# Attention heads on one Trainium2 core: lower weights in half units, probability copies ahead of the exponentials

## The chip, the cores and the metric

The kernel runs on one core of one Trainium2 chip. The metric is the device time of one execution in microseconds (us), and lower is better. TensorE (PE) multiplies, VectorE (DVE), ScalarE (ACT) and GpSimd (POOL) work on elements, SyncE (SP) issues most of the DMA transfers. Each engine takes its own instructions in program order and waits at semaphores for the others.

## The reference, cut to what matters

Two blocks of a network run over 256 tokens of 1024 channels in float32. The first block has a layer with two attentions of 16 heads each, both over the same normalised input. The first adds a forgetting bias to the scores, the second is a mixture of three dilated windows, which the kernel folds into one bias table. Its core is

```python
s = jnp.einsum('bqhd,bkhd->bhqk', q[:, q0:e], k[:, :e]).astype(f32) * scale
s = s + c[:, :, q0:e, None] - c[:, :, None, :e]
p = jax.nn.softmax(jnp.where(causal, s, NEG), axis=-1)
outs.append(jnp.einsum('bhqk,bkhd->bqhd', p.astype(v.dtype), v[:, :e]))
```

for the first one. All other layers (retention, a state space layer, a third attention of 8 heads, a feed-forward layer) are untouched by the change.

## The kernel before, in words

**Weights in two parts.** Float32 weights are multiplied as an upper and a lower part, each of which TensorE can take at full rate. The weights arrive in 232 units of 128x1024 elements (512 KB) in a ring of four buffers, `stage`. ACT copies a unit to `w_hi` with rounding (`split_hi`, line 607) and signals `hi_ready`. DVE subtracts that from the unit to make `w_lo` (`split_lo`, line 892) and signals `lo_ready`. SP loads unit u into a buffer when unit u - 4 has signalled `lo_ready`. TensorE takes three passes over each unit (lines 1507, 1511 and 1515 where the channels come out on the partitions, 1488, 1492 and 1496 where the tokens do), then signals `unit_used`.

**The two attention halves.** `for half in range(2)` runs the first attention and then the second, each with heads 0 to 15 of its own. The order is written out by hand on each engine.
- TensorE (`attend`): at an even head i it makes the scores of heads i + 2 and i + 3 (`scores_of_pair`, lines 1595 and 1596, a wait for `scored` of head i + 1 ahead of it). Then for each head i it turns the probabilities of head i by three transposes (line 1614; it waits for the exponentials of head i and for the copy of head i - 2), and then multiplies the values with the turned probabilities of head i - 1 (lines 1625 to 1627; it waits for the copy of head i - 1).
- DVE: for head i `score_max` adds the bias, writes `prob` and takes the row maximum (lines 1078 and 1079). It copies the turned probabilities of head i - 2 from PSUM into `prob_t` (`copy_prob`, line 1085) unless ACT does that head. At i = 9 and 17 it inverts the denominators, and at i = 11 and 19 it multiplies eight heads with the gate (line 1096), once POOL has scaled that gate (line 468). At i = 4, 8 and 12 it makes one lower unit each.
- ACT: for head n it takes the exponentials in two instructions (lines 708 and 709), and then copies the turned probabilities of head n - 2 if that is one of heads 0, 2, 6 and 10 (`copy_prob_act`, line 717). After head 2 it makes one more upper unit.

The values of the unit ahead of an attention are finished before its first turn. `prob` has three buffers, `prob_t` has two, and `copy_prob_act(n)` also waits until the values of head n - 2 are multiplied.

After an attention half TensorE goes straight on: after the first with the chunks `("qb", c)`, four units each, after the second with the turns of `turn_wide` (line 1444) and the output projection.

Of the kernel before, what the change touches and what calls it, by code (L numbers as in the profile page):

```python
# [20 lines left out]
F32 = mybir.dt.float32  # L21
# [3 lines left out]
ALU = mybir.AluOpType  # L25
# [21 lines left out]
RING = 4  # L47
UNIT = 1024
# [1 line left out]
NC = S // STEP  # L50
AHEAD = 3
DOWN_LAST = 3
SPLIT_HEADS = (4, 8, 12)
COPIED_BY_ACT = (0, 2, 6, 10)
MASKS_AT, TABLES_AT = 20, 42
FORGET_AT, PARAMS_AT = 5, 12
# [77 lines left out]
def build(nc, t):  # L134
    chunks, n_units = weight_chunks()
    number = {name: c[3] for name, c in chunks.items()}
    last_unit = {name: c[0] + c[1] - 1 for name, c in chunks.items()}

    with ExitStack() as ctx:
# [4 lines left out]
        stage = sb("stage", [P, RING, UNIT])  # L144
        w_hi = sb("w_hi", [P, RING, UNIT], F32R)
        w_lo = sb("w_lo", [P, RING, UNIT], F32R)
# [101 lines left out]
        def bank(b, width=BANK, at=0):  # L248
            return ps[:, b * BANK + at:b * BANK + at + width]
# [3 lines left out]
        hi_ready, lo_ready, unit_used = sem("hi_ready"), sem("lo_ready"), sem("unit_used")  # L253
# [38 lines left out]
        def result(name, width=BANK):  # L292
            if name[0] == "down":
                at = (4 + 2 * name[1]) * BANK
                return ps[:, at:at + 2 * BANK].rearrange("p (b n) -> p b n", b=2)
            n = number[name]
            return ps[:, (n % 2) * 2 * BANK:(n % 2) * 2 * BANK + 2 * BANK].rearrange("p (b n) -> p b n", b=2)[:, :, 0:width]

        def chunk_done(eng, name):

            eng.wait_ge(unit_used, last_unit[name] + 1)
# [296 lines left out]
        def _(act):  # L598
            next_unit = [0]
# [10 lines left out]
            def ahead(name):  # L610
                split_hi(last_unit[name] + 1 + AHEAD)
# [74 lines left out]
            for half, kind in enumerate(("ga", "gb")):  # L686
                for c in range(2):
# [3 lines left out]
                    for b in range(NB):  # L691
                        ins = nc.scalar.activation(gate0[half][:, b, c * 512:(c + 1) * 512], result((kind, c))[:, b, :], ACT.Silu, scale=rstd[:, b:b + 1])
# [11 lines left out]
            def exponentials(n):  # L704

                act.wait_ge(scored, n + 1)
                e = prob[:, n % 3, :]
                nc.scalar.activation(e[:, 0:256], e[:, 0:256], ACT.Exp, bias=neg_max[:, 1, n:n + 1], scale=-1.0, accum_out=den[:, 1, n:n + 1])  # L708
                nc.scalar.activation(e[:, 256:384], e[:, 256:384], ACT.Exp, bias=neg_max[:, 0, n:n + 1], scale=-1.0,
                                     accum_out=den[:, 0, n:n + 1]).then_inc(exped, 1)  # L710

            def copy_prob_act(n):

                act.wait_ge(prob_turned, n + 1)
                if n >= 2:
                    act.wait_ge(pv_done, n - 1)
                nc.scalar.activation(prob_t[:, n % 2, :], bank(2 + n % 2, 384), ACT.Copy).then_inc(prob_copied_act, 1)

            for half in range(2):
                v = "va" if half == 0 else "vb"  # L720
                if half == 1:
                    for part in range(2):
                        ahead((("qb", "kb")[part], 1))
                        act.wait_ge(b_turned, part + 1)
                        if part:
                            act.wait_ge(c_pow_ready, 1)
                        for i in range(4):
                            nc.scalar.activation(b_turn[:, 2 * part + i // 2, i % 2], bank(4 + i).rearrange("p (t n) -> p t n", t=CT), ACT.Copy).then_inc(b_ready, 1)
                for c in range(2):
                    if c == 0:  # L730
                        ahead((v, 0))
                    else:
                        split_hi(last_unit[(v, 1)] + AHEAD)
                        exponentials(16 * half)
                        exponentials(16 * half + 1)
                    chunk_done(act, (v, c))
                    for b in range(NB - c):
                        ins = nc.scalar.activation(v0[:, b, c * 512:(c + 1) * 512], result((v, c))[:, b, :], ACT.Copy, scale=rstd[:, b:b + 1])
                    ins.then_inc(drain_sem((v, c)), 1)
                for n in range(16 * half + 2, 16 * half + 16):  # L740
                    exponentials(n)
                    if copied_by_act(n - 2):
                        copy_prob_act(n - 2)
                    if n == 16 * half + 2:
                        ahead((v, 1))
            hi_of_wide(range(4))
# [11 lines left out]
            for c in range(4):  # L758
                ahead(("rv", c))
                chunk_done(act, ("rv", c))  # L760
                for b in range(NB):
                    ins = nc.scalar.activation(v1[:, b, c * 512:(c + 1) * 512], result(("rv", c))[:, b, :], ACT.Copy, scale=rstd[:, 2 + b:3 + b])
                ins.then_inc(drain_sem(("rv", c)), 1)
            for c in range(4):
                ahead(("rg", c))
                chunk_done(act, ("rg", c))
                for b in range(NB):
                    ins = nc.scalar.activation(gate1[:, b, c * 512:(c + 1) * 512], result(("rg", c))[:, b, :], ACT.Silu, scale=rstd[:, 2 + b:3 + b])
# [20 lines left out]
            for b in range(NB):  # L789
                ins = nc.scalar.activation(qkv[:, b, 0:SINK_H, :], result(("sq", 0))[:, b, :].rearrange("p (h d) -> p h d", d=HD), ACT.Copy,  # L790
                                           scale=rstd_in_q[:, b:b + 1])
            ins.then_inc(drain_sem(("sq", 0)), 1)
            chunk_done(act, ("skv", 0))
            for b in range(NB):
# [3 lines left out]
                ins = nc.scalar.activation(qkv[:, b, V_AT:V_AT + KV_H, :], heads[:, KV_H:2 * KV_H, :], ACT.Copy, scale=rstd_in[:, b:b + 1])  # L798
# [45 lines left out]
            for c in range(2):  # L844
                for b in range(NB):
                    act.wait_ge(mixed_ready, 2 * c + b + 1)
                    half = slice(c * 512, (c + 1) * 512)
# [22 lines left out]
            for b in range(NB):  # L870
                ins = nc.scalar.activation(down_out[:, b, 0:512], result(("down", 0))[:, b, :], ACT.Copy, scale=rstd[:, 14 + b:15 + b])
# [13 lines left out]
        def _(dve):  # L885
            next_unit = [0]

            def split_lo(until):

                for u in range(next_unit[0], min(until, n_units)):  # L890
                    dve.wait_ge(hi_ready, u + 1)
                    nc.vector.tensor_tensor(w_lo[:, u % RING, :], stage[:, u % RING, :], w_hi[:, u % RING, :].bitcast(F32), ALU.subtract).then_inc(lo_ready, 1)  # L892
                next_unit[0] = max(next_unit[0], min(until, n_units))

            def ahead(name):
                split_lo(last_unit[name] + 1 + AHEAD)
# [68 lines left out]
            for a in range(2):  # L965
                r = slice(a * SSM_N, (a + 1) * SSM_N)
                ins = nc.vector.tensor_copy(sp["ldt"][r, :], log_dt[r, :].rearrange("p (t a) -> p t a", a=2)[:, :, a])
# [57 lines left out]
            for i, (f0, f1, op) in enumerate(((fr_b, fi_b, ALU.subtract), (fi_b, fr_b, ALU.add))):  # L1025
                TT(b_tmp[0][:], b_in[0][:], f0, ALU.mult)
                then(TT(b_tmp[1][:], b_in[1][:], f1, ALU.mult))
                for a in range(2):
                    r = slice(a * SSM_N, (a + 1) * SSM_N)
                    ins = TT(b_wide[i][r, :, a, :], b_tmp[0][r], b_tmp[1][r], op)  # L1030
# [67 lines left out]
            for half in range(2):  # L1098
                if half == 1:
                    for c in range(2):  # L1100
                        take_heads("qb", q0, c)
                for c in range(2):
                    take_heads(("ka", "kb")[half], k0, c)
                v = (("va", "vb")[half], 1)
                split_lo(last_unit[v] + 1)
                for i in range(16 + 4):
                    n = 16 * half + i
                    if i < 16:
                        score_max(n, half)
                    if i == 1:  # L1110
                        chunk_done(dve, v)
                        TS(v0[:, 1, 512:1024], result(v)[:, 1, :], rstd[:, 1:2], None, ALU.mult).then_inc(v_block_ready, 1)
                    if 2 <= i < 18 and not copied_by_act(n - 2):
                        copy_prob(n - 2)
                    if i % 8 == 1 and i >= 9:
                        invert((n - 9) // 8)
                    if i % 8 == 3 and i >= 11:
                        if n == 35:
                            lo_of_wide(range(1))
                        gate_heads((n - 11) // 8)  # L1120
                    if i in SPLIT_HEADS:
                        split_lo(last_unit[v] + 2 + SPLIT_HEADS.index(i))

            def out_and_turn(kind, n_hi, gain):

# [25 lines left out]
            for kind, dst in (("rq", q1), ("rk", k1)):  # L1151
                for c in range(2):
# [3 lines left out]
                    for hh in range(2):  # L1156
# [5 lines left out]
                        ins = TT(by_sin, src, rot[:, 1, :].unsqueeze(1).to_broadcast([P, 2, S]), ALU.mult)  # L1162
                        then(ins)
                        TT(dst[:, h, 0, :], by_cos[:, 0, :], by_sin[:, 1, :], ALU.subtract)
                        ins = TT(dst[:, h, 1, :], by_sin[:, 0, :], by_cos[:, 1, :], ALU.add)
# [56 lines left out]
            for b in range(NB):  # L1222
                ins = STT(x[:, b, :], x[:, b, :], rstd[:, 4 + b:5 + b], row_a[:], ALU.mult, ALU.mult)
# [42 lines left out]
            for pair in range(2):  # L1266
                chunked = lambda v, m: v.rearrange("p (m n j) -> p m n j", m=m, j=STEP)
                ins = TT(u_p[:, 2 * pair:2 * pair + 2].rearrange("p m j n -> p m n j"), chunked(result(("u", 0))[:, pair, :], 2),
                         chunked(rstd_row[:], 1).to_broadcast([P, 2, NC, STEP]), ALU.mult)
# [32 lines left out]
            for b in range(NB):  # L1302
                ins = TT(y_attn[:, b, :].rearrange("p (h d) -> p h d", d=HD), bank(4 + b).rearrange("p (h d) -> p h d", d=HD),
                         inv_den[:, b, 32:40].unsqueeze(2).to_broadcast([P, SINK_H, HD]), ALU.mult)
# [8 lines left out]
            for c, dst in ((1, gate_z), (0, ssm_out)):  # L1313
                ahead(("glu", c))
                chunk_done(dve, ("glu", c))
                for b in range(NB):
                    ins = TT(dst[:, b, :], result(("glu", c))[:, b, :], row_b[:, c * 512:(c + 1) * 512], ALU.add)
# [83 lines left out]
            for b in range(NB):  # L1401
# [4 lines left out]
                for c in range(2):  # L1406
                    half = slice(c * 512, (c + 1) * 512)
# [539 lines left out]
```

## Time and profile before

| | |
|---|---|
| time, median of 3 runs | 804.79 us |
| lowest and highest | 803.68 and 807.3 us |
| the profiled execution | 803.58 us |
| its span | 801.8 us |
| TensorE busy | 776.6 us (97%) |
| VectorE busy | 519.9 us (65%) |
| ScalarE busy | 406.1 us (51%) |
| GpSimd busy | 218.0 us (27%) |
| granted TensorE clock, mean | 0.996 |

The span is the time from the first to the last instruction that the profiler saw, and the execution's own time has 1.8 us more around it. Busy shares are averages over stages that differ, so what matters for a change is which engine is waited for inside the stage that it touches.

### The profile page before, as it was taken

How to read it: one execution, taken by the hardware profiler on the slowest of the kernel's cores; microseconds unless marked ns; L12 is line 12 of the kernel's file. 1: busy time of each engine (PE TensorE's matmuls, PEld its weight loads, DVE VectorE, ACT ScalarE, POOL GpSimd, SP SyncE). 2: the span in 40 equal slices, each digit the busy share in tenths (PEclk: the TensorE clock that was granted, in tenths of full speed). 3: DMA queues.
4: the chain of work that ended last, by engine and by line, in shares of the span. 5: the costliest groups of instructions: out<-in, count | busy, mean ns of one | idle time of the engine just before them, and what ended most of it. 6: DMA issues, size and time to landing. Idle time of an engine off the chain costs nothing.

```text
span 801.8 us, 12695 instructions
## 1 busy us (share of the span) xinstructions
PE 776.6 (97%) x5133; PEld 678.5 (85%) x5133; DVE 519.9 (65%) x759; ACT 406.1 (51%) x649; POOL 218.0 (27%) x180
## 2 busy tenths in 40 slices
PE   7999999999989999999999999998999999999996
PEld 6879987899878889997777888987887888888885
DVE  4755864775547656875556975686678767677453
ACT  5653436534456445343435454726766655556441
POOL 3031893290531000018007930125102110111010
PEclk9999999999999999999999999999999999999999
DMA  8996993567721463656455466440263666665651
GB/s 217 214 256 205 217 206 106 124 160 180 157 79 58 147 194 109 227 165 184 127 159 160 150 205 197 137 150 7 83 233 122 196 208 189 186 184 179 213 180 53
DMA packets 77821, 130.72 MB, mean 163 GB/s; under 512 B 4414, under 2 KB 28210, under 8 KB 77634
## 3 DMA queue, kind: packets, MB, share of 16 engines
q1 hardware_dynamic: 76418, 125.00, 54.2%
q0 software_dynamic: 1200, 4.83, 2.1%
q8 instruction: 41, 0.67, 0.3%
q14 instruction: 18, 0.15, 0.1%
q10 hardware_dynamic: 144, 0.07, 0.0%
HBM read 128.82 MB, written 1.06 MB: 162 GB/s over the span
## 4 chain that ended last, share of the span: by engine, by line
PE 87%; DVE 4%; ACT 4%; DMA 3%; issue 1%; SPq 0%; POOL 0%; DVEq 0%; POOLq 0%; ACTq 0%
PE ps L1488 13%; PE ps L1492 13%; PE ps L1496 13%; PE ps L1528 10%; PE ps L1507 6%; PE ps L1511 6%; PE ps L1515 6%; PE ps L1532 5%; DMA stage<-in_even_w_in 3%; PE ps L1595 2%; PE ps L1614 1%; DVE w_lo L892 1%; ACT w_hi L607 1%; PE ps L1625 1%; PE ps L1905 1%
## 5 line engine op out<-in xcount | busy, mean ns | idle before, releaser
L892 DVE TENSOR_TENSOR w_lo<-stage,w_hi 128x1024 fp32r<-128x1024 f32 x232 | 303.7, 1327 | 166.3 <-ACT w_hi L607 165.8
L607 ACT ACTIVATE w_hi<-stage 128x1024 fp32r<-128x1024 f32 x232 | 242.6, 1061 | 238.1 <-PE ps L1496 112.3
L1488 PE MATMUL ps<-w_hi,act_t 128*128 128x512 f32 (+1 forms) x376 | 103.3, 398 | 3.3 <-issue 2.8
L1496 PE MATMUL ps<-w_lo,act_t 128*128 128x512 f32 (+1 forms) x376 | 98.6, 385 | 0.0
L1528 PE MATMUL ps<-act_t,w_hi 128*128 128x512 f32 x352 | 88.3, 393 | 0.7 <-DVE act_t L929 0.7
L1488 PEld LDWEIGHTS ps<-w_hi,act_t 128*128 128x128 f32 x376 | 68.6, 190 | 18.7 <-issue 5.8
L1492 PE MATMUL ps<-w_hi,act_t 128*128 128x512 f32 (+1 forms) x312 | 82.2, 387 | 0.0
L1496 PEld LDWEIGHTS ps<-w_lo,act_t 128*128 128x128 f32 x376 | 69.7, 188 | 14.3
L1528 PEld LDWEIGHTS ps<-act_t,w_hi 128*128 128x128 f32 x352 | 63.3, 189 | 12.2 <-issue 0.9
L1492 PEld LDWEIGHTS ps<-w_hi,act_t 128*128 128x128 f32 x312 | 58.2, 190 | 12.1
L1507 PE MATMUL ps<-act_t,w_hi 128*128 128x256 f32 x416 | 58.8, 284 | 0.0
L1511 PE MATMUL ps<-act_t,w_hi 128*128 128x256 f32 x416 | 58.4, 283 | 0.0
L1515 PE MATMUL ps<-act_t,w_lo 128*128 128x256 f32 x416 | 58.4, 283 | 0.0
L1507 PEld LDWEIGHTS ps<-act_t,w_hi 128*128 128x128 f32 x416 | 53.8, 193 | 0.2
L1515 PEld LDWEIGHTS ps<-act_t,w_lo 128*128 128x128 f32 x416 | 53.7, 193 | 0.0
L1511 PEld LDWEIGHTS ps<-act_t,w_hi 128*128 128x128 f32 x416 | 53.7, 193 | 0.0
L1532 PEld LDWEIGHTS ps<-act_t,w_lo 128*128 128x128 f32 x352 | 48.0, 190 | 3.5
L1532 PE MATMUL ps<-act_t,w_lo 128*128 128x256 f32 x352 | 49.1, 282 | 0.0
L584 POOL TENSOR_TENSOR big<-big 128x512 f32<-128x512 f32 x11 | 14.3, 1299 | 105.5 <-ACT big L864 105.5
L1492 PE MATMUL ps<-w_hi,y_lo 128*128 128x512 f32 x128 | 34.2, 389 | 0.0
L708 ACT ACTIVATE prob<-prob,neg_max 128x256 f32<-128x256 f32 x40 | 20.2, 506 | 22.5 <-DVE neg_max L1079 22.3
L1492 PEld LDWEIGHTS ps<-w_hi,y_lo 128*128 128x128 f32 x128 | 24.0, 188 | 5.0
(363 smaller groups left out, 1159.6 us busy)
## 6 DMA issues: line engine op xcount, KB each, us to landing
stage<-in_even_w_in SPq DMA_DIRECT2D x64, 512.0 KB, 5.5
stage<-in_odd_w_in SPq DMA_DIRECT2D x48, 512.0 KB, 4.3
stage<-in_w_gate_up SPq DMA_DIRECT2D x44, 512.0 KB, 4.7
stage<-in_w_down SPq DMA_DIRECT2D x22, 512.0 KB, 4.0
stage<-in_even_w_out SPq DMA_DIRECT2D x16, 512.0 KB, 4.3
stage<-in_odd_w_out SPq DMA_DIRECT2D x16, 512.0 KB, 4.6
stage<-in_w_in SPq DMA_DIRECT2D x10, 512.0 KB, 4.5
stage<-in_w_out SPq DMA_DIRECT2D x8, 512.0 KB, 4.7
```

Of the source, the lines that this page charges most:

```text
L607: nc.scalar.activation(w_hi[:, u % RING, :], stage[:, u % RING, :], ACT.Copy).then_inc(hi_ready, 1)
L708: nc.scalar.activation(e[:, 0:256], e[:, 0:256], ACT.Exp, bias=neg_max[:, 1, n:n + 1], scale=-1.0, accum_out=den[:, 1, n:n + 1])
L892: nc.vector.tensor_tensor(w_lo[:, u % RING, :], stage[:, u % RING, :], w_hi[:, u % RING, :].bitcast(F32), ALU.subtract).then_inc(lo_ready, 1)
L1488: mm(out[:, b, :], a_hi(k)[:, tok[b]], hi[:, i, :], start=(k == 0), stop=False)
L1492: mm(out[:, b, :], a_lo(k)[:, tok[b]], hi[:, i, :], start=False, stop=False)
L1496: ins = mm(out[:, b, :], a_hi(k)[:, tok[b]], lo[:, i, :], start=False, stop=(k == k_tiles - 1))
L1507: mm(out[m], columns(hi[:, i, :], m), act_t[:, k, :], start=(k == 0 and m % 2 == 0), stop=False, skip_group_check=True)
L1511: mm(out[m], columns(hi[:, i, :], m), act_t[:, KD + k, :], start=False, stop=False, skip_group_check=True)
L1515: ins = mm(out[m], columns(lo[:, i, :], m), act_t[:, k, :], start=False, stop=(k == k_tiles - 1), skip_group_check=True)
L1528: mm(out[m], hi[:, i, w[m]], both[:, :, k, :], start=(k == 0), stop=(k == KD - 1), skip_group_check=True)
L1532: ins = mm(out[m][:, 0, :], lo[:, i, w[m]], act_t[:, k, :], start=False, stop=(k == KD - 1), skip_group_check=True)
L1595: even = mm(bank(0, width, at), qs[0][:, tok], ks[0][:, 0:width], start=True, stop=True)
```

## The change

The three whole lower units of each attention half become six half units. Each is 512 of the 1024 columns. They stand at the ends of heads 4, 5, 7, 9, 12 and 13 in place of 4, 8 and 12, and only the second half of a unit signals `lo_ready`. On ACT the copy of head n - 2 moves ahead of the exponentials of head n.

```diff
-SPLIT_HEADS = (4, 8, 12)
+SPLIT_HEADS = (4, 5, 7, 9, 12, 13)
...
                 for n in range(16 * half + 2, 16 * half + 16):
-                    exponentials(n)
                     if copied_by_act(n - 2):
                         copy_prob_act(n - 2)
+                    exponentials(n)
                     if n == 16 * half + 2:
                         ahead((v, 1))
...
+            def split_lo_half(u, part):
+
+                half = slice(part * UNIT // 2, (part + 1) * UNIT // 2)
+                dve.wait_ge(hi_ready, u + 1)
+                ins = nc.vector.tensor_tensor(w_lo[:, u % RING, half], stage[:, u % RING, half], w_hi[:, u % RING, half].bitcast(F32), ALU.subtract)
+                if part == 1:
+                    ins.then_inc(lo_ready, 1)
+                    next_unit[0] = u + 1
...
                     if i in SPLIT_HEADS:
-                        split_lo(last_unit[v] + 2 + SPLIT_HEADS.index(i))
+                        at = SPLIT_HEADS.index(i)
+                        split_lo_half(last_unit[v] + 1 + at // 2, at % 2)
```

## Rows read from the trace of the kernel before

**Rows 1.** The page: its head, and section 4, the chain that ended last.
```profile
span 801.8 us, 12695 instructions
...
PE 87%; DVE 4%; ACT 4%; DMA 3%; issue 1%; SPq 0%; POOL 0%; DVEq 0%; POOLq 0%; ACTq 0%
```

**Rows 2.** Windows: the first attention and what follows; columns PE, PEld, DVE, ACT, POOL.
```profile
131.30:158.70 27.40, 23.77 (x203) 21.01 (x203) 19.80 (x75) 17.77 (x63) 3.69 (x4) 1.00 0.44 97
158.70:231.20 72.50, 72.50 (x522) 67.97 (x522) 39.96 (x38) 30.08 (x40) 38.56 (x25) 1.00 0.65 153
```

**Rows 3.** Waits, 131 to 159 us: total us, times, longest.
```profile
PE ps L1625 <- ACT prob_t L717: 3.6, 4, 1.2
```

**Rows 4.** The chain, 126 to 160 us, first attention: start us, us, what.
```profile
131.31 0.41 PE ps L1595
...
132.20 0.43 PE ps L1614 x3
...
135.17 0.41 PE ps L1595
...
139.02 0.41 PE ps L1595
...
139.88 0.48 PE ps L1614 x3
...
140.97 0.34 PE ps L1614 x3
...
141.96 0.41 PE ps L1595
...
148.75 0.41 PE ps L1595
...
152.84 0.41 PE ps L1595
...
158.67 1.01 PE ps L1507 x8
```

**Rows 5.** Timeline of ACT, 126 to 145 us: start us, us, instruction, idle before.
```profile
132.87 0.51 ACT L708 ACTIVATE prob<-prob,neg_max 128x256 f32<-128x256 f32 x1 [0.84 <-DVE neg_max L1079]
...
134.13 1.04 ACT L607 ACTIVATE w_hi<-stage 128x1024 fp32r<-128x1024 f32 x1
...
136.73 0.51 ACT L708 ACTIVATE prob<-prob,neg_max 128x256 f32<-128x256 f32 x1 [0.68 <-DVE neg_max L1079]
...
137.62 0.46 ACT L717 ACTIVATE prob_t<-ps 128x384 f32<-128x384 f32 x1
```

**Rows 6.** Timeline of DVE, both attentions.
```profile
136.05 0.42 DVE L1078 CUSTOM_DVE_ANT_0 prob<-ps,big 128x256 f32<-128x256 f32 x1 [2.08 <-PE ps L1596]
...
136.61 1.22 DVE L892 TENSOR_TENSOR w_lo<-stage,w_hi 128x1024 fp32r<-128x1024 f32 x1
137.75 0.42 DVE L1078 CUSTOM_DVE_ANT_0 prob<-ps,big 128x256 f32<-128x256 f32 x1
...
138.30 0.55 DVE L1085 COPY prob_t<-ps 128x384 f32<-128x384 f32 x1
...
148.75 1.22 DVE L1096 TENSOR_TENSOR gate_a<-ps,gate_a 128x1024 f32<-128x1024 f32 x1
...
259.70 0.69 DVE L935 TENSOR_TENSOR y_lo<-ps,act_t 128x512 fp32r<-128x512 f32 x1 [1.89 <-ACT act_t L660]
```

**Rows 7.** The chain, 226 to 260 us, second attention.
```profile
231.16 0.41 PE ps L1595
...
258.59 1.43 PE ps L1444 x13
```

**Rows 8.** Timeline of POOL: the scaling of the first gate.
```profile
145.95 1.90 POOL L468 TENSOR_TENSOR gate_a<-gate_a,inv_den 128x1024 f32<-128x1024 f32 x1 [19.23 <-DVE inv_den L1089]
```

**Rows 9.** Timeline of DVE after the first attention.
```profile
161.12 4.09 DVE L892 TENSOR_TENSOR w_lo<-stage,w_hi 128x1024 fp32r<-128x1024 f32 x2
```

**Rows 10.** DMA issues, 128 to 165 us: KB each, median us to landing.
```profile
stage<-in_even_w_in SPq DMA_DIRECT2D x4, 512.0 KB, 4.8
```

## The prediction

> **What bounds the kernel now.** I read the page's chain first: TensorE holds 87% of it [rows 1], so time can only come out of the places where TensorE itself waits. The windows show such a place. In the 27.4 us of the first attention TensorE is busy 23.77 us, and in the 72.5 us behind it 72.50 of 72.50, at a granted clock of 1.00 in both [rows 2]. The list of waits names the cause of nearly all of it: the values of line 1625 waited four times, 3.6 us in all, for ACT's copy of turned probabilities [rows 3]. Four is the number of heads that ACT copies (0, 2, 6 and 10).
>
> The chain in order of time gives the size. Take the start of each pair of score matmuls as a clock tick [rows 4]. A pair in which ACT copies nothing lasts 141.96 - 139.02 = 2.94 us, all of it TensorE's own work. The ticks that hold an ACT copy are longer: 135.17 - 131.31 = 3.86, 139.02 - 135.17 = 3.85, and 152.84 - 148.75 = 4.09. From 141.96 to 148.75 lie 6.79 us, which is a free pair and one of 3.85. Then 5.83 us of tail lead to 158.67.
>
> The engine timelines say why. In the second pair the turn of head 2 ends at 135.17 + 0.86 + 0.48 = 136.51 (scores 139.88 - 139.02 = 0.86, turn 0.48 [rows 4]). DVE's maximum of head 4 ends a little later, ACT goes into the exponentials of head 4 at 136.73 and reaches the copy of head 2 only at 137.62 [rows 5]. The copy was ready to go 1.1 us earlier. TensorE has the turn of head 3 to do meanwhile, then it stands.
>
> **The reorder.** Put ahead of the exponentials, the copy starts when the turn ends, about 136.55, and takes some 0.42 us to its signal (0.46 less what overlaps, [rows 5]). That is 136.97, while TensorE wants it after values 1 and turn 3, at 136.51 + (140.97 - 139.88 - 0.48 = 0.61) + 0.34 = 137.46 [rows 4]. So the wait is gone with 0.5 us to spare. It is paid by the exponentials of head 4, which start at about 136.97 in place of 136.73. They are needed by the turn of head 4, after the next scores (138.1 + 0.86), and take 0.9 us (136.73 to 137.62 [rows 5]), so the 0.24 us is covered.
>
> Per pair of the first attention, with the ticks as they would fall:
> - Heads 0 and 1: the turn of head 0 ends at 132.63 [rows 4], its copy at about 133.05, and turn 1 at about 133.0. The values run 133.09 to about 133.98, where before they ended at 135.17. Saved: 1.19 us.
> - Heads 2 and 3: ACT's exponentials 2 now start at 133.05, 0.18 later than 132.87, but the upper unit behind them no longer has the 0.37 us copy ahead of it, so it starts at about 133.94 in place of 134.13 [rows 5]. Exponentials 3 then end about 135.8, and turn 3 wants them at 133.98 + 0.86 + 0.48 + 0.61 = 135.93. Tick 2.94 in place of 3.85. Saved: 0.91 us.
> - Heads 6 and 7: the same, 0.91 us. Heads 10 and 11: 4.09 - 2.94 = 1.15 us. There the copy also stood behind exponentials that had waited for the gate on DVE (148.75, 1.22 us [rows 6]); now it needs only the turn.
>
> Sum: 1.19 + 0.91 + 0.91 + 1.15 = 4.16 us. New ticks: 131.31, 133.98, 136.92, 139.86, 142.80, 145.74, 148.68, end 154.51.
>
> **The half units.** TensorE's next scores also wait for the maximum of the odd head, and a whole lower unit stands ahead of it. DVE's pitches are 0.56 us for a maximum (136.05 to 136.61), 1.14 for a unit (136.61 to 137.75), and 0.47 for a copy (0.55 less the same 0.08 of overlap) [rows 6]. With the whole unit that maximum would end at tick + 0.86 + 0.03 + 0.56 + 1.14 + 0.56 = tick + 3.15, later than 2.94: 0.21 us lost in the pairs of heads 4 and 8. In the pair of head 12 the gate ends first, at 146.9 by the new ticks, 0.25 after the scores, so 0.46. That makes 0.9 us per attention. The reorder alone would therefore bring 4.16 - 0.9 = 3.3 per attention, 6.5 us in all. The half units alone would bring about nothing, since the copy behind the exponentials would still end last.
>
> The trace has no half unit. Bounds: not under half of the 1.14, 0.57, and not over 0.69, the busy time of a 128x512 subtraction [rows 6]. I take 0.61 (0.69 less 0.08). The odd maximum then ends at tick + 2.62, and in the pair of head 12 at 146.9 + 0.56 + 0.61 + 0.56 = 148.63, against a wish at 148.68. That is the tightest place, with 0.05 us. A pair's work on DVE is 2 x 0.56 + 2 x 0.47 + 0.61 = 2.67, under 2.94. The extra 0.08 us per unit lies in DVE's idle time.
>
> One rule of the Trainium skill speaks against this edit. "VectorE: DVE Perf Modes", section "The TRN2 errata — SBUF-src ops pay a fixed extra latency per instruction", says that every instruction pays a fixed latency and small tiles pay it each time. By its formula two halves take 1.38 us against 1.22 for one whole; the trace's 0.69 and 1.22 for these widths agree [rows 6]. By the page the sum changes by 0.1 us at head 12.
>
> One half unit stands beside POOL's scaling of the gate, which starts when DVE's reciprocal at head 9 is done and takes 1.90 us [rows 8]. Two units made right after the attention, with POOL at work, took 4.09 / 2 = 2.04 us each [rows 9], so this one may cost up to 0.6 us more. Behind it the maximum of head 11, wanted by the next scores, has 2.94 - 0.89 - 0.56 - 0.47 - 0.56 = 0.46 us to spare. Cost taken: none, at most 0.2.
>
> **The second attention** has the same order and length, 258.59 - 231.16 = 27.43 against 158.67 - 131.31 = 27.36 [rows 4, 7]. Another 4.16. Total 8.3 us. I take off 0.1 for the tight spots: 8.2.
>
> **Does it stay saved?** What follows is TensorE without a gap [rows 2]. Its inputs shift with it: POOL's work there starts at DVE's reciprocal of this same attention. The sum against the profiled execution gives 803.58 - 8.2 = 795.4 us. That execution lies 1.2 under the median of the runs, so on the median it is 804.79 - 8.2 = 796.6; I say 796.5.
>
> **The rivals.**
> - *DVE becomes the bound* (14%). If half units cost nearly as much as whole ones, for instance 1.1 us beside other work, the odd maximum ends at tick + 3.11, and each pair with a half unit runs 0.2 to 0.5 us over. Over six such places that is 1.5 us per attention, a gain of 5.3 and 799.5 us. For it: a unit can take 2.04 [rows 9]. Against it: inside the attention the whole units took 1.22 with POOL idle.
> - *Swallowed later* (8%). A stage behind, bound by POOL or by a load, waits for something that did not move, and less than 4 us stay: 801 to 805 us, 803.5 say. Against it: 72.50 of 72.50.
> - *Slower: the ring runs dry* (4%). The third lower unit is finished at head 13 in place of 12, and SP loads the unit four further only then. Place: the third unit of `("qb", 1)`. By the new ticks `lo_ready` comes at about 149.7, 4.8 us before the attention's end. The load lands 4.8 us later [rows 10], at 154.5. A unit lasts 3 x 0.96 = 2.9 us, so TensorE wants it at 154.5 + 6 x 2.9 = 171.9. It decides only if a load takes over 22 us; loads of 26 us in both halves would cost more than is saved, 804.79 + 4 = 809 us. There is nothing near that in the trace.
> - The forecast itself, 74%.
>
> **Range.** The likeliest case spans 795 to 798 (the median of a few runs can fall 1.2 under or 1 over the forecast). The DVE rival reaches 799.8. I give 794.9 to 799.9. Runs of this kernel can't tell less than 0.5% (4 us) from no change. Faster by more than 0.5% (under 800.8) holds the forecast and the DVE rival: 0.88. Same: most of the swallowed case, 0.08. Slower: 0.04.
>
> **What would show it.** Right: ticks of 2.9 us in all pairs of lines 1595, some 23.2 us per attention, and the wait of line 1625 for line 717 at nearly zero. ACT's line 717 starts within 0.1 us of the turn's end. Six `w_lo` of 128x512 per attention, near 0.69 us each. Wrong, if a new wait of line 1595 for DVE's line 1079 appears (half units too dear), if turns at line 1614 wait for exponentials (the reorder made them late), or if the attentions are shorter and TensorE gained an idle stretch between 155 and 231 us.

## The result, and the profile after

The changed kernel takes 798.38 us (median of 4 runs, 795.69 to 798.7) against 805.32 us for the kernel before (4 runs, 803.68 to 807.3). The ratio is 0.9886, with a 95% interval of 0.9845 to 0.9927. A second comparison gave 798.62 us (6 runs) against 806.66 (20 runs), ratio 0.9895, interval 0.9868 to 0.9923. The change makes the kernel about 1.1% faster, which is 6.9 us in the first comparison and 8.0 in the second. The forecast was 796.5 us, in a range of 794.9 to 799.9.

The page after, head, busy times and the engines of the chain:

```profile
span 796.8 us, 12701 instructions
...
PE 777.4 (98%) x5133; PEld 680.7 (85%) x5133; DVE 522.9 (66%) x765; ACT 405.6 (51%) x649; POOL 220.3 (28%) x180
...
PE 88%; DVE 4%; DMA 3%; ACT 2%; issue 1%; SPq 0%; POOL 0%; DVEq 0%; POOLq 0%; ACTq 0%
```

The windows over the first attention, what follows, and the second attention (columns as in [rows 2]):

```profile
134.00:157.40 23.40, 23.00 (x201) 20.82 (x201) 19.99 (x78) 17.50 (x63) 3.78 (x4) 1.00 0.51 114
157.40:230.00 72.60, 72.60 (x524) 68.09 (x523) 40.00 (x38) 30.07 (x40) 38.72 (x25) 1.00 0.65 153
230.00:253.40 23.40, 22.97 (x201) 20.76 (x201) 20.00 (x78) 16.50 (x62) 2.65 (x2) 1.00 0.21 70
```

TensorE now stands still for 0.4 us of an attention where it stood still for 3.6 [rows 2]. The waits, 131 to 155 us, have turned round: 3.6 us of TensorE waiting for ACT [rows 3] became 0.3, and ACT now waits for TensorE's turns.

```profile
ACT prob_t L717 <- PE ps L1624: 2.2, 3, 0.7
...
PE ps L1635 <- ACT prob_t L717: 0.3, 1, 0.3
```

The score ticks in TensorE's timeline, first attention (start us, us, instruction; every second row of a pair is left out). The distances are 2.87, 3.07, 2.93, 2.90, 2.94, 3.04 and a tail of 5.70:

```profile
133.90 0.48 PE L1605 MATMUL ps<-k,q 64*128 64x256 f32 x1
...
136.77 0.48 PE L1605 MATMUL ps<-k,q 64*128 64x256 f32 x1
...
139.84 0.48 PE L1605 MATMUL ps<-k,q 64*128 64x256 f32 x1
...
142.77 0.48 PE L1605 MATMUL ps<-k,q 64*128 64x256 f32 x1
...
145.67 0.48 PE L1605 MATMUL ps<-k,q 64*128 64x256 f32 x1
...
148.61 0.48 PE L1605 MATMUL ps<-k,q 64*128 64x256 f32 x1
...
151.65 0.48 PE L1605 MATMUL ps<-k,q 64*128 64x256 f32 x1
...
157.35 0.84 PE L1517 MATMUL ps<-act_t,w_hi 128*128 128x256 f32 x5
```

**Where the time went.** All ticks below are read in this one way, from TensorE's timeline, for both kernels. (The chain of [rows 4] dates the same matmuls some 0.07 us later.) An attention runs from its first tick to the end of its tail. It took 27.24 and 27.34 us before, and takes 23.45 and 23.48 after: 3.79 + 3.86 = 7.65 us less. What lies between the two attentions took 72.61 us in both of these profiles, and what lies behind them 543.4 in both. (Two further profiles of the changed kernel took longer behind them; see the experiments.) The spans differ by only 801.8 - 796.8 = 5.0 us because this execution reached its first tick 2.66 us later, at 133.90 in place of 131.24. That is ahead of anything the change touches. TensorE's clock was lower there, 0.93 and 0.90 of full speed in the mean (columns as above):

```profile
40.00:60.00 20.00, 15.87 (x71) 13.04 (x70) 10.16 (x11) 10.24 (x12) 8.51 (x8) 0.93 1.03 254
60.00:80.00 20.00, 20.00 (x154) 20.00 (x154) 11.79 (x19) 7.20 (x8) 1.39 (x3) 0.90 0.62 169
```

The first tick lies anywhere from 129.7 to 135.3 us in the profiles of this study, so single spans can't be compared to within 5 us. The ticks can, where the clock is the same.

### The profile page after: what moved, and what is told of

Same layout as the page of the kernel before. It is cut to its first block, busy times and chain, and to the rows that moved or that the text cites. A ratio compares the mean times of both kernels' runs of the same rounds, so it can differ in the third digit from the quotient of the medians.

```text
span 796.8 us, 12701 instructions
## 1 busy us (share of the span) xinstructions
PE 777.4 (98%) x5133; PEld 680.7 (85%) x5133; DVE 522.9 (66%) x765; ACT 405.6 (51%) x649; POOL 220.3 (28%) x180
## 3 DMA queue, kind: packets, MB, share of 16 engines
HBM read 128.82 MB, written 1.06 MB: 163 GB/s over the span
## 4 chain that ended last, share of the span: by engine, by line
PE 88%; DVE 4%; DMA 3%; ACT 2%; issue 1%; SPq 0%; POOL 0%; DVEq 0%; POOLq 0%; ACTq 0%
PE ps L1498 13%; PE ps L1502 13%; PE ps L1506 13%; PE ps L1538 10%; PE ps L1517 6%; PE ps L1521 6%; PE ps L1525 6%; PE ps L1542 5%; DMA stage<-in_even_w_in 3%; PE ps L1605 2%; PE ps L1624 2%; DVE w_lo L892 1%; PE ps L1636 1%; PE ps L1637 1%; PE ps L1915 1%
## 5 line engine op out<-in xcount | busy, mean ns | idle before, releaser
L892 DVE TENSOR_TENSOR w_lo<-stage,w_hi 128x1024 fp32r<-128x1024 f32 x226 | 299.0, 1342 | 165.0 <-ACT w_hi L607 164.4
```

## The experiments

Each is given with what was expected of it. This is what the ticks of all of them showed (in us; the six pairs begin with the scores of heads 2, 4, 6, 8, 10 and 12, and a pair is named by them here; "first" and "second" are the two attentions with their tails, which take about 5.7 in most of them):

| kernel | pairs of the first attention | first | second |
|---|---|---|---|
| before | 3.86, 3.85, 2.94, 3.86, 2.93, 4.10 | 27.24 | 27.34 |
| changed | 2.87, 3.07, 2.93, 2.90, 2.94, 3.04 | 23.45 | 23.48 |
| changed, again | 2.86, 3.07, 2.93, 2.90, 2.94, 3.05 | 23.44 | 23.48 |
| reorder only | 2.86, 3.35, 2.93, 3.35, 2.93, 3.58 | 24.70 | 24.79 |
| halves only | 3.86, 4.48, 2.94, 3.86, 2.94, 4.09 | 27.86 | 27.32 |
| whole units at odd heads | 2.87, 3.07, 2.98, 2.90, 3.17, 2.89 | 23.72 | 23.81 |
| more DVE work | 2.87, 3.40, 3.50, 2.90, 4.69, 3.64 | 27.26 | 32.33 |
| upper unit later | 2.87, 2.90, 2.93, 2.90, 2.93, 3.05 | 23.28 | 23.38 |
| DVE copies all | 2.94, 3.28, 2.93, 2.94, 2.93, 3.51 | 24.24 | 24.33 |
| both later | 2.87, 2.90, 2.94, 2.90, 2.93, 2.90 | 23.14 | 23.28 |

**The changed kernel again.** No edit.

> The changed kernel once more, as the yardstick for the three runs beside it. Each attention took 23.45 and 23.48 us from its first score tick to the end of its tail, where the kernel before took 27.24 and 27.34, so 7.65 us should be gone: about 797.5 us against 805. If instead the first comparison was helped or hurt by the start of the execution (the profiled one reached the attention 2.66 us later than the one of before), the attentions keep their 23.5 us and only the time ahead of the first score tick differs.

Measured: 798.62 us against 806.66, and 23.44 and 23.48 us per attention. So the attentions repeat within 0.01 us. The rest of the execution does not. Its first tick was at 129.71, 4.2 us earlier than in the first profile, and yet its span is 796.6 us against 796.8: what lies behind the attentions took 547.4 us where the kernel before and the first profile had 543.4. TensorE stood still for 2 us ahead of line 1506 with nothing in the profile to release it, and then ran 6 us at a mean granted clock of 0.72:

```profile
525.34 0.85 PE L1506 MATMUL ps<-w_lo,act_t 128*128 128x512 f32 x3 [1.98 <-issue]
```

The same gap, 0.46 to 2.15 us long, is in five of the eight profiles of this study with half units (two of the three of the changed kernel, the half units alone, more DVE work, both later), and in none of the five with whole units. The clock fell behind it only here and in the run with more DVE work; here the gap and the lower clock make up 3.0 of the 4 us. Whether the half units have a part in the gap stays open.

**The reorder without the half units.**

```diff
                 for n in range(16 * half + 2, 16 * half + 16):
-                    exponentials(n)
                     if copied_by_act(n - 2):
                         copy_prob_act(n - 2)
+                    exponentials(n)
```

> ACT's copy ahead of the exponentials, whole lower units at heads 4, 8 and 12 as before. The prediction's theory: the odd maximum behind a whole unit is late by 0.2 us in the pairs of heads 4 and 8 and by 0.46 in that of head 12, so an attention takes 0.9 us more than with half units, 24.3 us, and some 1.8 us of the 7.65 are missing: about 799.5 us. Rival A, the half units are what frees the scores: the reorder alone gives little and each attention stays above 26 us. Rival B, the half units do nothing: 23.5 us each.

Measured: 801.56 us (9 runs), ratio 0.9938 (0.9913 to 0.9963), 24.70 and 24.79 us. The reorder alone brings 2.54 + 2.55 = 5.1 us of the 7.65, and the half units behind it the other 1.25 + 1.31 = 2.6. Both rivals fall. TensorE now waits for DVE's maximum at the end of the second, fourth and sixth tick, and DVE's timeline of the second shows the whole unit between the even maximum and the odd one:

```profile
140.88 0.48 PE L1595 MATMUL ps<-k,q 64*128 64x256 f32 x1 [0.21 <-DVE neg_max L1079]
...
147.16 0.48 PE L1595 MATMUL ps<-k,q 64*128 64x256 f32 x1 [0.37 <-DVE neg_max L1079]
...
153.67 0.48 PE L1595 MATMUL ps<-k,q 64*128 64x256 f32 x1 [0.61 <-DVE neg_max L1079]
```

```profile
138.49 0.42 DVE L1078 CUSTOM_DVE_ANT_0 prob<-ps,big 128x256 f32<-128x256 f32 x1 [1.10 <-PE ps L1596]
...
139.05 1.22 DVE L892 TENSOR_TENSOR w_lo<-stage,w_hi 128x1024 fp32r<-128x1024 f32 x1
140.19 0.42 DVE L1078 CUSTOM_DVE_ANT_0 prob<-ps,big 128x256 f32<-128x256 f32 x1
```

The forecast had 3.15 us for the second and fourth tick, and they took 3.35. The chain of DVE work is as reckoned, but of the two handovers around it the first was set at 0.03 and the second left out: from the end of the scores at 137.53 + 0.86 to DVE's start at 138.49 pass 0.10 us, and from the end of the odd maximum at 140.19 + 0.56 to the next scores at 140.88 pass 0.13.

**The half units without the reorder.** In the changed kernel the two calls on ACT are put back.

```diff
                 for n in range(16 * half + 2, 16 * half + 16):
+                    exponentials(n)
                     if copied_by_act(n - 2):
                         copy_prob_act(n - 2)
-                    exponentials(n)
```

> Half units, the copy behind the exponentials as before. The prediction's theory: the values still wait four times for ACT's copy, an attention takes 27.2 us plus or minus 0.2, no difference in time. Rival A (the half units free the scores): an attention falls by 1 us or more, 803 us or less.

Measured: 806.75 us (12 runs) against 806.66, ratio 0.9998 (0.9977 to 1.0019). Its second attention took 27.32 us. As expected, the half units bring nothing while the copy is last. The second tick of the first attention, 4.48 us, was not expected; it is taken up below.

**Whole units, moved to odd heads.** Reorder only, and

```diff
-SPLIT_HEADS = (4, 8, 12)
+SPLIT_HEADS = (5, 9, 13)
```

> The reorder with whole lower units, moved from the even heads 4, 8 and 12 to the odd heads 5, 9 and 13, where no odd maximum stands behind them in the same pair. If it is the place of a unit that costs (between an even maximum and its odd one) and not its length, an attention takes 23.5 us, as with half units, within 0.2. If it is the length (DVE's work of a pair, 2 x 0.56 + 2 x 0.47 + 1.14 = 3.2, is over 2.94), each of the three pairs runs 0.25 us over and it takes 24.2.

Measured: 799.83 us (6 runs), ratio 0.9913 (0.9887 to 0.9938), 23.72 and 23.81 us. Against the changed kernel the whole units at 5 and 13 cost 0.05 and 0.14 us in the first attention and the one at head 9 0.23, and the pair of head 12, which now has none, is 0.15 shorter. So it is mostly the place of a unit that cost, not its length: moving the units gives 0.98 us per attention, where halving them gave 1.25 and 1.31, with no new instruction.

**More work on DVE.** Ahead of each half unit stands one more instruction. Nothing reads what it writes.

```diff
+                nc.vector.tensor_reduce(out=spare[:, extra[0] - 1:extra[0]], in_=stage[:, u % RING, half], axis=mybir.AxisListType.X, op=ALU.max)
                 ins = nc.vector.tensor_tensor(w_lo[:, u % RING, half], stage[:, u % RING, half], w_hi[:, u % RING, half].bitcast(F32), ALU.subtract)
```

> The changed kernel with one more instruction ahead of each half unit: DVE takes the maximum of the same 128x512 of stage into a spare column, which nothing uses. It adds some 0.6 us of DVE work to each of the 12 half units and leaves ACT and TensorE alone. It prices the rival in which half units are dear. By the ticks the odd maximum of the pairs of heads 4 and 12 comes 0.6 us later, which is 0.3 and 0.55 past the wish, and the extra work of heads 5, 7, 9 and 13 uses up 0.2 to 0.3 us of idle DVE time each and runs over by 0.3: 1.5 to 2.2 us more per attention, 25.0 to 25.7 us. If DVE had more slack than I counted, less than 0.5 us more.

Measured: 822.57 us in one run. The first attention took 27.26 us, 3.8 more, where 1.5 to 2.2 were expected. The fifth tick, 4.69 us in place of 2.94, holds most of the surprise. The half unit at head 9 now came just after the start of POOL's gate scaling in place of just before it, and ended 0.55 us behind it (150.74 against 150.19), as if it had waited for the whole of it. DVE's and POOL's timelines:

```profile
148.06 0.63 DVE L903 TENSOR_REDUCE spare<-stage 128x1 f32<-128x512 f32 x1
148.61 2.13 DVE L904 TENSOR_TENSOR w_lo<-stage,w_hi 128x512 fp32r<-128x512 f32 x1
```

```profile
148.29 1.90 POOL L469 TENSOR_TENSOR gate_a<-gate_a,inv_den 128x1024 f32<-128x1024 f32 x1 [17.86 <-DVE inv_den L1103]
```

In the changed kernel the half unit starts first and POOL's instruction is the one that grows, to 2.16 us, which nobody waits for:

```profile
145.80 0.63 DVE L899 TENSOR_TENSOR w_lo<-stage,w_hi 128x512 fp32r<-128x512 f32 x1
```

```profile
146.03 2.16 POOL L468 TENSOR_TENSOR gate_a<-gate_a,inv_den 128x1024 f32<-128x1024 f32 x1 [17.45 <-DVE inv_den L1098]
```

By the Trainium skill ("SBUF — State Buffer", section "SBUF: two separate sides") a VectorE instruction with two SBUF inputs and a GpSimd instruction that reads SBUF take one pair of ports exclusively, and whichever starts first keeps it for its whole length. The rows of the two half units and the two scalings agree: the one that starts first takes its usual 0.63 or 1.90 us, the other one longer.

The second attention took 32.33 us. Its half unit at head 9 took 2.13 us too. TensorE was busy 1.38 of 3 us while it waited there, and then its granted clock fell to 0.50, the level of 1.2 GHz, for the rest of the attention:

```profile
250.00:253.00 3.00, 1.38 (x13) 1.09 (x12) 3.00 (x12) 1.70 (x7) 0.14 (x1) 1.00 0.32 106
253.00:256.00 3.00, 3.00 (x21) 2.86 (x17) 3.00 (x10) 1.64 (x7) 0.00 (x0) 0.58 0.21 79
...
262.00:265.00 3.00, 3.00 (x16) 3.00 (x16) 0.76 (x2) 0.00 (x0) 0.00 (x0) 0.50 0.00 0
```

**The upper unit later.** In the changed kernel:

```diff
-                    if n == 16 * half + 2:
+                    if n == 16 * half + 4:
                         ahead((v, 1))
```

> The changed kernel with ACT's upper unit made after head 4 in place of head 2. The second tick of the changed kernel is 3.07 us where 2.94 were forecast. If exponentials 3 and copy 2 behind the upper unit are the cause, that tick falls to 2.94 and the attention to 23.3 us. If it stays at 3.07, the turn and the values themselves are longer there.

Measured: 796.18 us in one run. The second tick fell from 3.07 to 2.90 us and the attentions to 23.28 and 23.38. In the changed kernel ACT's timeline had the upper unit at 136.68, exponentials 3 at 137.62 and the copy of head 2 only at 138.50, though the turn of head 2 had ended at about 138.0 (TensorE went on to the next values then). So the reorder still leaves one copy behind work that isn't urgent.

```profile
136.68 1.04 ACT L607 ACTIVATE w_hi<-stage 128x1024 fp32r<-128x1024 f32 x1
137.62 0.50 ACT L708 ACTIVATE prob<-prob,neg_max 128x256 f32<-128x256 f32 x1
...
138.50 0.47 ACT L717 ACTIVATE prob_t<-ps 128x384 f32<-128x384 f32 x1
```

**All copies on DVE.** In the changed kernel:

```diff
-COPIED_BY_ACT = (0, 2, 6, 10)
+COPIED_BY_ACT = ()
```

> The changed kernel with no copy on ACT in the two attention halves: DVE copies all 16 heads. It asks whether ACT's copies are needed once nothing on ACT holds them up. DVE's work of the pair of head 4 becomes 2 x 0.56 + 2 x 0.47 + 2 x 0.61 = 3.28 and its odd maximum ends at tick + 0.89 + 0.56 + 0.47 + 0.61 + 0.56 = 3.09, so pairs 4 and 12 run over by 0.15 to 0.5 us, others not: 23.5 to 24.5 us per attention. If the handover between ACT and TensorE was itself the dear part, it falls under 23.3.

Measured: 799.74 us in one run, 24.24 and 24.33 us, with 3.28 and 3.51 us in the pairs of heads 4 and 12 where the others took 2.93 or 2.94. ACT's copies are still worth 0.8 us per attention. But an attention with half units and none of these copies is also 3.0 us shorter than one with half units and the four copies in their old place (24.33 against 27.32, the second attentions): there, the copies on ACT did harm.

**Both later.** The upper unit after head 4, and

```diff
-SPLIT_HEADS = (4, 5, 7, 9, 12, 13)
+SPLIT_HEADS = (4, 5, 7, 9, 13, 15)
```

> The changed kernel with both of its remaining longer ticks attacked: ACT's upper unit after head 4 (which took the second tick from 3.07 to 2.90 us) and the third lower unit's halves at heads 13 and 15 in place of 12 and 13, so that no half unit stands behind the gate in the pair of head 12. That tick should fall from 3.05 to 2.93, the others stay, and an attention takes 23.2 to 23.3 us against 23.45: 0.2 us per attention, 0.4 us in all, which the time itself can't show. If the third lower unit at head 15 is too late for what follows, the tail or the first chunk behind the attention grows instead.

Measured: 797.11 us (6 runs) against 806.64, ratio 0.9892 (0.9861 to 0.9922), 23.14 and 23.28 us. By the ticks this is the version to keep: 0.51 us less in the attentions than the changed kernel. The times can't tell the two apart.

**Three further profiles, for the clock.** No edit.

> The kernel before, profiled once more, for the spread of its runs (802.5 to 810.9 us in 20) against that of the changed kernel (795.2 to 799.8 in 6). In the run with half units alone the granted clock stood at 0.50 for some 3 us right after TensorE's wait for the first copy, and the tick was 4.48 us in place of 3.86. If the waits of the old order let the clock fall now and then, one or both of these two profiles show a stretch at 0.50 inside an attention, and a tick over 4.1. If not, all ticks are those of the first profile, and the spread comes from the start of the execution.

> As the run beside it: the kernel before, a further profile, same question. A stretch at a granted clock of 0.50 inside an attention, with a tick over 4.1 us, or the 27.3 us per attention of the first profile.

> The changed kernel, a further profile for the same question. Its longest wait for a copy is some 0.3 us, so no stretch below 1.00 should lie inside an attention: 23.4 to 23.5 us each, whatever the start of the execution takes.

Measured: the kernel before took 27.87 and 27.32 us in one of them (an execution of 807.29 us), and 35.17 and 27.32 in the other, with ticks of 3.86, 4.52, 5.40, 5.40, 5.40 and 4.89 in its first attention. The windows of that second one:

```profile
134.00:137.00 3.00, 1.73 (x18) 1.32 (x14) 1.94 (x10) 2.16 (x7) 0.00 (x0) 1.00 0.00 0
137.00:140.00 3.00, 3.00 (x22) 2.77 (x21) 1.87 (x6) 2.33 (x10) 0.00 (x0) 0.71 0.00 0
140.00:161.00 21.00, 21.00 (x103) 18.87 (x101) 11.25 (x42) 8.19 (x33) 2.97 (x3) 0.50 0.42 101
```

For 21 us the granted clock stood at 0.50, and that execution took 813.58 us. The changed kernel took 23.45 and 23.48 us again, in an execution of 802.00 us. Its clock fell elsewhere, in the third attention:

```profile
555.00:560.00 5.00, 5.00 (x70) 4.88 (x74) 1.50 (x8) 3.67 (x11) 2.64 (x4) 0.50 0.02 3
```

Behind its two attentions it took 547.7 us, where all three profiles of the kernel before took 543.4. In the 5 us ahead of that fall TensorE was busy 3.61 us; the kernel before was busy 3.75 of 5 us at the same stage and kept 1.00. So this stage can lose some 4 us whose cause no run here settles.

## Why the prediction was right

**What bounded it: right.** TensorE waited for ACT's copies, four times per attention. Taking the copy out of its place behind the exponentials took the wait away (3.6 us to 0.3); the halves alone did nothing.

**The reorder: right, its size too large.** Forecast 4.16 us per attention with half units; measured 3.79 and 3.86. Three terms are off. The first tick saved 0.99 in place of 1.19: the copy starts 1.51 us after the tick (133.90 to 135.41) where 1.39 was reckoned (131.24 to 132.63), since no handover from TensorE to ACT was counted, and the values follow 0.55 us behind its start (135.41 to 135.96) where 0.46 was reckoned. The second saved 0.78 in place of 0.91, because exponentials 3 and the copy stand behind the upper unit; the forecast checked the turn of head 3 against that, and not the copy of head 2 behind it, which started at 138.50, some 0.4 us after its turn, where the forecast's own sign asked for 0.1. The sixth saved 1.06 in place of 1.15; it is the tight spot behind the gate, and it went to 2.90 when no half unit stood there. The fourth saved 0.96, a little more than 0.91, since a pair with ACT's copy runs 2.90 us. The reorder alone was forecast at 6.5 us in all and brought 5.1.

**The half units: right, their size too small.** They bring 2.6 us in all where 1.7 to 1.8 were forecast, since of the handovers between TensorE and DVE (0.10 and 0.13 us) only 0.03 was priced. So the two parts are off in opposite directions, and the sum, 8.2 us against 7.65, is closer than either of them. That is luck: the reorder alone brought 1.4 us less than forecast and the half units 0.9 more. The duration of a half unit was forecast at 0.69 us, from a subtraction that reads PSUM, and they took 0.67 in the mean (12 of them, 8.1 us). The meeting with POOL cost nothing, as taken, but only by the order of two starts, 0.23 us apart; the forecast had reckoned with at most 0.6 us there and a half unit that came second took 1.5 us more.

**It stays saved: right between the attentions, open behind them.** Between them lie 72.61 or 72.62 us in all thirteen profiles, so the ring did not run dry. Behind them the changed kernel took 543.4, 547.4 and 547.7 us in its three profiles, and the kernel before 543.4 in all three of its own. The medians, 6.9 and 8.0 us lower, don't show a swallowed gain of that size as the rule; the profiles are too few to rule it out in some executions. The rival of DVE as the bound is real at 0.6 us more per half unit, as the run with more DVE work showed, and steeper than it was priced.

**The median.** It came out 1.9 us above the forecast. The ticks account for 0.55 of that, and the kernel before was itself 0.5 us higher in its four runs than in the three that the forecast started from. The rest is not traced.

**Left out.** The waits of the old order can also let the clock fall. The sum of 8.2 us against the profiled execution knew nothing of it, for that profile had 1.00 in both attentions.

## What to carry to other kernels

On an engine that takes its instructions in order, put the short one that another engine waits for ahead of the long one with slack, and look at what else stands ahead of it: here the reorder gave 5.1 us and one upper unit still held 0.2 us. Place a background instruction where nobody waits for what follows it, before you cut it up: moving three whole units gave three quarters of what halving them gave. Compare such edits by the distances between repeated instructions in the trace, which repeat within 0.01 us in the three profiles of the changed kernel, while the start of the execution varied by over 5 and what follows the attentions by over 4. Look at the granted clock of each stretch first: in the kernel before the same six ticks took 7.9 us more once the clock had fallen.

## What the runs showed of the hardware that was not expected

- TensorE's granted clock fell to 0.50 behind a wait of 1.24 us, in some profiles and not in others. The first copy's wait in the old order leaves TensorE busy 1.73 of 3 us (in 134 to 137 of the second further profile of the kernel before), and in three of four profiles with that order the clock then stood at 0.50 in the first attention: for some 3 us twice (ticks of 4.48 and 4.49 in place of 3.85), and for over 21 us once, which cost 35.17 - 27.24 = 7.9 us. In the fourth, the first profile, the same wait of 1.24 us (1.72 of 3 busy in 132 to 135) left it at 1.00. In the second attention, whose first wait is 1.33 us long, it never fell in these four. The other eight profiles, without copies behind the exponentials and without added work, had no fall in either attention. So the link with the wait is likely, but what decides was not found.
- Whether this is why the runs of the old order spread more (802.5 to 810.9 us in 20 and 803.1 to 814.8 in 11, and 803.3 to 810.3 in 12 with half units, against 795.2 to 799.8 in 6 for the changed kernel, with 802.0 in a single run) was not settled, as only a profile shows the clock of a stretch. By it the gain of the change in the median could be over the 7.65 us of its ticks; it was 6.9 in the first comparison and 8.0 in the second.
- For these 21 us TensorE was busy 21.00 of 21 us at 0.50, with turns, scores and values only, and did not get back to 1.00. In the run with more DVE work it was as busy (3.00 of 3 us) at 0.50 up to the end of the second attention.
- One half unit of 0.68 us took 2.13 us when POOL's instruction had started 0.32 us before it (148.29 against 148.61), and 0.63 us when it started 0.23 us before POOL's (145.80 against 146.03).
